# Adding the two halves of the row sums of squares on VectorE before the products that spread them over the partitions

## What is computed

```python
def rms_norm(x, g):
    xf = x.astype(jnp.float32)
    y = xf * lax.rsqrt(jnp.mean(xf * xf, axis=-1, keepdims=True) + EPS)
    return (y * g.astype(jnp.float32)).astype(x.dtype)

for l in range(DEPTH):                     # DEPTH = 2
    h = rms_norm(x, norm1_g[l])            # norms 0 and 2
    proj = h @ w_in[l]                     # 7 kinds of columns, three token mixers, gates
    ...                                    # gMLP, latent attention, gated DeltaNet
    x = x + merged @ w_out[l]
    h2 = rms_norm(x, norm2_g[l])           # norms 1 and 3
    x = x + jnp.square(jax.nn.relu(h2 @ w_ff1[l])) @ w_ff2[l]
```

## Time and profile before

| | us |
|---|---|
| median of 3 runs (1763.12 to 1763.38) | 1763.38 |
| profiled execution | 1764.11 |
| its span, first to last instruction | 1762.3 |
| PE busy in it | 1744.1 |
| DVE busy | 958.8 |
| ACT busy | 689.9 |
| POOL busy | 1066.3 |

### The profile page before, as it was taken

The page is one execution under the profiler, slowest core; times in us unless marked ns, Lnnn a source line. Parts: engine busy times, 40 slices in busy tenths (PEclk is TensorE's granted clock), DMA queues, the critical chain, the costliest instruction groups (busy, mean ns, idle before and its releaser), DMA issues.

```text
span 1762.3 us, 26300 instructions
## 1 busy us (share of the span) xinstructions
PE 1744.1 (99%) x10006; PEld 1426.3 (81%) x10006; DVE 958.8 (54%) x1565; ACT 689.9 (39%) x1241; POOL 1066.3 (61%) x572
## 2 busy tenths in 40 slices
PE   8999999999999999999999999999999999999999
PEld 7778888778888888888787788887788888888887
DVE  6786636653542455444576866266443435444445
ACT  6433316650104444444355243075411054444442
POOL 6444367235665777777774434662456657777776
PEclk9999999999999999999999999999999999999999
DMA  6222133123235666666542222331332356666655
GB/s 201 85 69 77 49 96 108 37 96 96 84 97 169 157 172 161 161 174 157 130 156 78 71 70 61 96 96 37 108 96 85 97 158 163 159 173 158 169 154 144
DMA packets 58897, 207.18 MB, mean 118 GB/s; under 512 B 6369, under 2 KB 8705, under 8 KB 58785
## 3 DMA queue, kind: packets, MB, share of 16 engines
q1 hardware_dynamic: 47520, 164.94, 29.9%
q0 software_dynamic: 9216, 33.56, 10.2%
q10 hardware_dynamic: 2048, 7.10, 1.1%
HBM read 184.61 MB, written 4.19 MB: 107 GB/s over the span
## 4 chain that ended last, share of the span: by engine, by line
PE 95%; ACT 2%; DVE 2%; issue 1%; DMA 0%; SPq 0%; DVEq 0%; ACTq 0%
PE ps L662 22%; PE ps L664 22%; PE ps L663 22%; PE ps L1259 6%; PE ps L1261 6%; PE ps L1260 6%; PE ps L1131 2%; PE ps L1140 1%; PE ps L1153 1%; PE ps L681 1%; PE ps L904 1%; PE ps L891 0%; DMA xin<-x 0%; PE ps L941 0%; PE ps L1203 0%
## 5 line engine op out<-in xcount | busy, mean ns | idle before, releaser
L662 PE MATMUL ps<-hHi,wHi 128*128 128x512 f32 x1360 | 553.2, 407 | 1.3 <-DVE convd L1916 1.3
L664 PE MATMUL ps<-hHi,wLo 128*128 128x512 f32 x1360 | 530.4, 390 | 0.0
L663 PE MATMUL ps<-hLo,wHi 128*128 128x512 f32 x1360 | 529.8, 390 | 0.0
L562 POOL TENSOR_SCALAR wHi<-wraw 128x1024 fp32r<-128x1024 f32 x168 | 181.4, 1080 | 497.3 <-PE ps L664 480.2
L567 POOL TENSOR_TENSOR wLo<-wraw,wHi 128x1024 fp32r<-128x1024 f32 x168 | 415.2, 2472 | 13.9
L593 POOL TENSOR_TENSOR wLo<-w,wHi 128x1024 fp32r<-128x1024 f32 x96 | 239.2, 2514 | 138.6 <-ACT wHi L1690 138.0
L662 PEld LDWEIGHTS ps<-hHi,wHi 128*128 128x128 f32 x1360 | 255.4, 188 | 61.5 <-issue 6.9
L663 PEld LDWEIGHTS ps<-hLo,wHi 128*128 128x128 f32 x1360 | 255.7, 188 | 54.7 <-issue 3.8
L664 PEld LDWEIGHTS ps<-hHi,wLo 128*128 128x128 f32 x1360 | 255.3, 188 | 54.2
L1259 PE MATMUL ps<-wHi,fHi 128*128 128x512 f32 x448 | 174.8, 390 | 1.8 <-issue 1.8
L1260 PE MATMUL ps<-wLo,fHi 128*128 128x512 f32 x448 | 174.3, 389 | 0.0
(11 more groups left out here) (334 smaller groups left out, 2675.0 us busy)
## 6 DMA issues: line engine op xcount, KB each, us to landing
wraw<-stream SPq DMA_DIRECT2D x224, 512.0 KB, 3.6
w<-stream SPq DMA_DIRECT2D x64, 512.0 KB, 4.4
w<-w POOLq DMA_DIRECT2D x32, 512.0 KB, 6.9
b<-stream SPq DMA_DIRECT2D x16, 512.0 KB, 3.5
b<-stream POOLq DMA_DIRECT2D x16, 512.0 KB, 6.4
w<-stream POOLq DMA_DIRECT2D x16, 512.0 KB, 8.1
xin<-x SPq DMA_DIRECT2D x4, 512.0 KB, 6.8
y<-x ACTq DMA_DIRECT2D x1, 2048.0 KB, 9.9
```

The lines of the kernel that those rows point to most:

```text
L562: nc.gpsimd.tensor_scalar(wHi[:, slot], wraw[:, slot % RAW], 1.0, 0.0, ALU.mult, ALU.add).then_inc(unit_high, 1)
L662: mm(o, lh[lc], rh[rc], start=start, stop=False)
L663: mm(o, lh[lc], rl[rc], start=False, stop=False)
L664: return mm(o, ll[lc], rh[rc], start=False, stop=stop)
```

## The change

A new tile `rowsum` (128 partitions by 4) holds the sum of the two halves. DVE adds them in one instruction, `sum_rows`, as soon as all eight row sums of a norm are there; it also waits until the products of the norm before have read `rowsum`. `sum_stream` waits for the new semaphore `rows_summed` in place of `rows_squared` and makes one product for each `t`. `sum_rows` stands behind `stream_low(0)` in norm 0, behind `add_stream` of the second half in norms 1 and 3, and behind `stream_low` in norm 2. The pad `back` is left as it is.

```diff
-        rowsq = sb("rowsq", [P, 2, TT])
+        rowsq, rowsum = sb("rowsq", [P, 2, TT]), sb("rowsum", [P, TT])
...
                 def sum_stream(norm):
 
-                    pe.wait_ge(rows_squared, 8 * norm + 8)
+                    pe.wait_ge(rows_summed, norm + 1)
                     pe.wait_ge(h_lo, 8 * norm + 3)
                     for t in range(TT):
-                        for half in range(2):
-                            last = mm(S(2)[:, t * P:(t + 1) * P], rowsq[:, half, t:t + 1].broadcast_to([P, P]), ident, start=half == 0, stop=half == 1)
+                        last = mm(S(2)[:, t * P:(t + 1) * P], rowsum[:, t:t + 1].broadcast_to([P, P]), ident, start=True, stop=True)
                     last.then_inc(stat_summed, 1)
...
+            def sum_rows(norm):
+
+                dve.wait_ge(rows_squared, 8 * norm + 8)
+                if norm:
+                    dve.wait_ge(stat_summed, norm)
+                nc.vector.tensor_tensor(rowsum[:], rowsq[:, 0], rowsq[:, 1], ALU.add).then_inc(rows_summed, 1)
...
             zero_rows()
             stream_low(0)
+            sum_rows(0)
             dve.wait_ge(tables_in, 48)
...
                     add_stream(half, layer * per.sums_full, layer * per.unit_done + UNIT_NO[("out", 0)])
+                    if half:
+                        sum_rows(2 * layer + 1)
                     stream_low(2 * layer + 1, range(4 * half, 4 * half + 4))
...
                 if layer < DEPTH - 1:
                     stream_low(2 * layer + 2)
+                    sum_rows(2 * layer + 2)
```

More of the change, by code:

```diff
@@ L170 @@
     y_stored = 16; prm_loaded = 16; x_loaded = 16
-    h_lo = 16; h_high = 16; rows_squared = 16; stat_summed = 2; rl_done = 2; rstd_ready = 2
+    h_lo = 16; h_high = 16; rows_squared = 16; rows_summed = 2; stat_summed = 2; rl_done = 2; rstd_ready = 2
     act_tile = 12; csq_ready = 8; csq_summed = 2; ksum_copied = 2; ksum_turned = 2
@@ L329, in hybrid_trunk @@
         h_lo, h_high, rows_squared = sem("h_lo"), sem("h_high"), sem("rows_squared")
+        rows_summed = sem("rows_summed")
         stat_summed, rl_done, rstd_ready = sem("stat_summed"), sem("rl_done"), sem("rstd_ready")
```

## The result

The changed kernel takes 1783.22 us, the median of five runs (1777.75 to 1784.81), against 1763.38 before (1763.12 to 1764.77). That is 1.0103 times the time before, with a 95% interval of 1.0086 to 1.0120. The forecast was 1759.9 us in a range from 1759.5 to 1761.7. It was wrong by 23 us, and in the direction too. By the 0.2% of the prediction it is slower.

What follows compares the result with a forecast made beforehand. PE was taken as the bound, busy 1744.1 of 1762.3 us. Savings of 3.57 us less 0.1 for shifted tiles, additions costed at nothing, gave 3.47: median 1763.38 to 1759.9 us, range 1759.5 to 1761.7.

Steps and rivals of the forecast that it cites:

- the 0.2% of the prediction: Threshold on the whole kernel's time: 3.53 us, about what a measurement can tell from no change.
- What is removed: PE's line 690: four of eight products go in each of four norms, saving 0.89 us each, 3.57 in all.
- The two figures of the Trainium skill: Matmul issue gaps for 128 columns, about 56 and 81 ns, making the 32 removed records worth 1.8 or 2.6 us.
- What also changes, places in SBUF: Tiles behind the pad move 32 bytes; transfers of xin and the last store might slow, priced 0.1 us, bounds 0 to 0.9.
- rival 2: Transfers into tiles shifted 32 bytes take a share longer; 1768.4 us at half longer; chance 0.05 for above 0.2%.
- a DMA or an engine is slower at the shifted tiles: Listed sign of a wrong prediction, concerning the tiles moved 32 bytes; no size given for an engine.
- What is added: One DVE addition of 128x4 per norm, 163 ns by an existing row, costed at nothing because idle time covers it.
- a margin of 0.47 us: Norm 2, the tightest: PE may go on at 891.63, its first weight load started at 892.10; missing it costs up to 0.4.
- The cover of 3.2 us in norm 0: DVE's small tables, delayed behind the addition to 19.15 to 21.5, still finish 3.2 us before xrow, due at 24.77.
- What moves: After the norms: PE's later waits for DVE stay as long, other margins hold, so all four 0.89 us savings stand.
- Rival 1: Something fixed takes part back; 1761.6 us if norms 1 and 3 gave nothing; 0.18, shared with a 0.3 to 1.8 shift loss.
- rival 3: PE waits for the addition (1760.3 us) or lone products are no cheaper (1763.4); 0.07, shared with a no-change shift loss.

Runs made afterwards that it cites:

- e2: The kernel before with only the pad 32 bytes larger, so all shared tiles behind it move by 32 bytes: 1780.58 us, ratio 1.0094.
- e1: The changed kernel with the pad 32 bytes smaller, so the shared tiles behind it stand at their old places: 1768.89 us, ratio 1.0030.
- e5: The changed kernel with the shared tiles at their old places and norm 0's addition moved behind the rotation angles: 1762.98 us, ratio 1.0000.
- e6: The changed kernel with the shared tiles at their old places and norm 0 keeping eight products without an addition: 1760.77 us, ratio 0.9981.
- e7: The kernel before with one more wait: VectorE waits for norm 0's row sums ahead of the small tables: 1766.07 us, ratio 1.0018.
- e8: The changed kernel with only norm 0's addition moved behind the rotation angles, shared tiles still 32 bytes further on: 1776.70 us, ratio 1.0071.
- e12: The kernel before with wHi and wLo moved by 32 bytes, hHi, hLo and the tiles behind the pad unmoved: 1800.46 us, ratio 1.0208.
- e4: The kernel before with everything from hHi on, both operands of nearly every pass, moved by 32 bytes: 1765.19 us, ratio 1.0009.
- e3: The changed kernel with the shared tiles behind the pad 64 bytes past their old places: 1781.54 us, ratio 1.0105.

## Why the prediction was wrong

**What is removed: right.** 0.89 us a norm, 32 records, 8 in each block, within the bounds of 3.52 to 3.68. The proportion of line 690's own records, 8 x 0.1116 = 0.89, held. The two figures of the Trainium skill, which would have made it 1.8 or 2.6 us, don't fit this kernel's float32 products.

**What also changes, places in SBUF: the step that failed.** The prediction saw that the 32 bytes moved every tile behind the pad, and priced only transfers. That part was right, or nearly: the transfers `w<-w` land after 6.7 us in place of 6.9, and the loads of `xin` after 6.5 in place of 6.8. The engines' reads of the moved tiles weren't priced at all: the sum has 0.1 us for the place, with bounds of 0 and 0.9, and the rival beyond them, rival 2, reckons with transfers alone. 2400 passes of 6.4 ns more are 15.4 us, and e2 measured 16.8. Among its signs of being wrong the prediction did name "a DMA or an engine is slower at the shifted tiles", and that is the one that came, without a price. No row of the kernel before had one pass at both distances, so the size couldn't be read there. What could have been seen is that PE, busy for 99% of the span, reads two tiles in each pass, and that the change altered the distance of the two in 2400 passes. A bound for that belonged in the range. Rival 2 had the right edit and sign with the wrong mechanism, and gave 1768.4.

**What is added: mis-sized.** 0.16 us was taken from a row with one input in PSUM. The words "apart from the place of its operands" set aside what decided. With both inputs in SBUF it took 0.82 to 2.25 us in the changed kernel. For norms 1 to 3 the cover still held: PE shows no wait in front of line 690, and the step of 0.89 us is seen whole in e1, e5 and e6. In norm 2, with a margin of 0.47 us, it was close: the addition took 0.82 us there and ended at 901.09, and the first weight load of the block began at 901.17. From the start of the transposes to the block it is 8.96 us (892.59 to 901.55), against 8.95 before, so 0.01 us was lost at most. A longer POOL instruction at that moment would have been on the path.

**The cover of 3.2 us in norm 0: wrong.** The small tables were moved from 16.51 to 19.15 at their old durations, 2.4 us in all. In their old place POOL was waiting for a transfer; in the new one it was at work, and they took 13.4 us in e1 (18.84 to 32.25) and 11.7 in e7 (18.37 to 30.05). The rows that the margins were read from the earlier trace rows are of VectorE, ScalarE and TensorE. The row of POOL in the same stretch of the kernel before shows the collision, and the prediction doesn't use it:

```profile
18.95 1.05 POOL L562 TENSOR_SCALAR wHi<-wraw 128x1024 fp32r<-128x1024 f32 x1 [3.58 <-DMA wraw<-stream]
```

The late tables are worth 6.5 us (e8 against the changed kernel) or 5.9 (e5 against e1), with a wide spread.

The Trainium skill has this one. "GPSIMD Engine Reference", in its specifications, says that GpSimd's SBUF interfaces are shared with VectorE, in contention with VectorE's two-port modes or two SBUF inputs. "SBUF — State Buffer", in the section on SBUF's two separate sides, calls it an exclusive lock, held for the whole instruction by whichever engine starts first. The rows agree: `rowsum` took 2.25 us with two inputs and 0.16 with one, beside the same POOL instruction, line 568.

**What moves: right in three norms.** PE's later waits for `kqe` and `convd` stayed at 1.6 and 1.2 us. The prediction didn't see that a start that is shifted by a microsecond changes which VectorE and POOL instructions meet in the feed-forward part, 1.55 us each time.

**The account.** Between the two profiled executions the span grew by 16.0 us: 15.4 for the passes, 2.7 at the two waits for line 2347 in the feed-forward part, 1.5 in the first 14 us, less 3.6, which makes 16.0. In those first 14 us PE's passes followed each other at 0.43 us, against 0.23 from 9.9 in the kernel before (chain of the changed kernel):

```profile
9.93 0.43 PE ps L731
10.36 0.43 PE ps L730
```

0.43 us is also the pace of e1 at the lower level of the clock. The windows give 1.00 here, but they say so wherever the trace has no entry of the granted clock: its first entry, of 1.0, stands at 14.1 us in the changed kernel and at 8.4 in the kernel before, whose "1.0 over the whole span" therefore holds from 8.4 on. So the start most likely ran at the lower level, and for longer in the changed kernel. The first entry is at 14.8 us in e2 and 13.2 in e8, which start in the same way, and between 7.7 and 10.3 in all others, with and without the shift and the addition. Neither explains it, and why the clock rose late in three executions stays open. The late tables cost PE no wait in the profiled execution: they show in the three runs with the lower mean clock, and so in the median.

**The rivals and the chances.** Rival 1 and rival 3 didn't occur. The change does what it says, and no fixed wait took the saving. Slower had been given 0.05.

## What to carry to other kernels

A new tile of a few bytes moves every tile that is allocated behind it: keep the others' distances when you add one, above all where matrix products read from both sides of it, or take its bytes from the pad. In this kernel multiples of 256 bytes are the distances that are known to do. Before an instruction of VectorE is added or moved, look at what GpSimd runs at that moment, not only at whether VectorE is idle: the addition with two inputs in SBUF lasted as long as GpSimd's instruction, some casts and products with one did too, and the sum along an axis didn't. And a wait that is put ahead of independent work should be priced with that work at its new time.

## What the runs showed of the hardware

- A 128x512 pass of this kernel takes 227 ns when its two operands lie a multiple of 256 bytes apart, and 233 when they lie 32 bytes off that (e2, e12 and the changed kernel), whichever side was moved; both moved together, 227 (e4). 64 bytes off gives 227 to 233 (e3); 128 was not tried for them. This is shown for passes with `wHi` or `wLo` on one side; those on `rowsr` take 232 to 235 at a multiple of 256 too. Passes of 384 columns (174 ns) and float32 passes of 128 (109 ns) are the same at both. In the kernel before, with all distances right, some 400 of the 6,500 passes still took 230 to 244 ns, for a cause that stays open.
- VectorE's additions with two SBUF inputs, and also its casts and products from SBUF to SBUF in the angles, last until GpSimd's running instruction ends: 2.25, 2.07 and 2.43 us in place of 0.16, 0.17 and 0.20. One of 128x768 took 6.89 behind three GpSimd instructions in a row, in place of 0.95 to 1.98. Sums along the free axis took 0.16 us beside them, 11 of 11 times.
- After PE's stall at 53 to 55 us the granted clock was 0.55 in the 7 us that followed (e1), and the kernel went from 0.5 us ahead of the kernel before, at 52 us, to 6.6 behind at 59, for a wait of 4.5.
